# Depthwise convolution stage: shifted copies by way of HBM and 32-column matmuls for taps on VectorE and diagonal matmuls

## The chip, the cores and the metric

The kernel runs on one core of a Trainium2 chip. The metric is the device time of one execution, in microseconds (us), median of several runs. All data are float32.

## The reference, cut to what matters

The program is a chain of three small networks of 1024 features (D) over 256 tokens (T): SwiGLU blocks, several attention mixers, two mixtures of experts and one convolution block. Only the convolution block is changed. It stands between two SwiGLU blocks and adds its result to x:

```python
def rms_norm(x, g):
    y = xf * lax.rsqrt(jnp.mean(xf * xf, axis=-1, keepdims=True) + RMS_EPS)
    return y * g

def conformer_conv(h, w_pw1, b_pw1, w_dw, b_dw, ln_g, ln_b, w_pw2, b_pw2):
    val, gate = jnp.split(h @ w_pw1 + b_pw1, 2, axis=-1)
    u = val * jax.nn.sigmoid(gate)
    u = conv(u, w_dw, 31 taps, causal, one filter for each channel) + b_dw
    u = jax.nn.silu(layer_norm(u, ln_g, ln_b))
    return u @ w_pw2 + b_pw2

x = x + conformer_conv(rms_norm(x, g), ...)
```

## The kernel before, in words

x stays in SBUF with features on the partitions: 8 chunks (c) of 128 channels, 256 tokens along the free axis. The engines (TensorE `pe`, ScalarE `act`, VectorE `dve`, GpSimd `pool`, SyncE `sp`) each run their own hand-written order of work, stage by stage, and wait for each other by counting semaphores (class `Signal`).

Weights arrive in slabs of 128x2048 floats (1 MB). SyncE loads them all in one order into a ring of four (L2554); ScalarE rounds each into a high part (`round_slab`, L1352), VectorE subtracts to get the low part (`rest_slab`, L1771), and TensorE multiplies in three passes, high by high, high by low, low by high (`product`, L616 to L618), or in the SwiGLU blocks in two passes, the first with both parts of the input side by side (`product_wide`, L687 and L688). A slab can be rounded when TensorE has done with the slab three before it; both engines work two slabs ahead of TensorE. Where a slab is rounded in the order of ScalarE's and VectorE's other work is written out in each stage.

The convolution stage (`conv` of each engine) goes like this. VectorE first adds the last result of the block before to x (`finish`, L1893, once for each pair of chunks). ScalarE squares x, TensorE sums the squares over the partitions with a matrix of ones (L638), the root and its reciprocal follow (L1792, L1376, L1794), VectorE scales x (L1808), and the scaled input is split into a high part by ScalarE (L1383) and a low part by VectorE (`h_rest`, L1816). Eight slabs of w_pw1 follow (`project_slab`), each giving value and gate of one chunk in a PSUM bank; ScalarE takes the sigmoid (L1491) and VectorE makes the gated chunk u (L1997).

The 31 taps are shared out: chunks 0 to 4 go to VectorE, one 128x256 multiply-and-add for each tap (L2005 the first, L2008 the rest, 155 in all, up to 14 behind each projected slab and what is left after the last one). Chunks 5 to 7 go to TensorE as 93 matmuls of a diagonal 128x128 matrix with the shifted chunk (L866); ScalarE (L1497) and GpSimd (L2508) make the diagonals, two of three and one of three. When all is done TensorE sums the chunks for the mean (L871), VectorE subtracts it (L2019), ScalarE squares (L1504), TensorE sums again (L876), and the reciprocal root follows (L2021, L1506, L2023).

Each chunk is then scaled (L2026), put through SiLU (L1509), rounded (L1511) and its low part taken (L1816 again), one chunk after the other:

```python
for c in range(DC):
    nc.vector.tensor_tensor(v.v[:, c, :], v.v[:, c, :], v.stat[:, 1, :], ALU.mult).then_inc(k.scaled.up())
    self.h_rest(c, v.v[:, c, :], DC)
self.out_project(v, DC, "b_pw2")
```

`out_project` multiplies by w_pw2 in slabs of 256 output columns, so that each slab needs all eight chunks and finishes two chunks of x, to which VectorE adds them at once with the bias (L1831).

Three other stages already do what this change brings to the convolution. `early_input` (mixer and SwiGLU) splits the unnormed x times the gain, chunk by chunk behind `finish`, and leaves the scale by the root to the output; `add_squares` adds the squares on GpSimd so that TensorE sums only two tiles; and `mixed_half` with `add_down` multiplies by slabs of 256 input rows, so that TensorE starts with the first chunk, all eight PSUM banks are filled together and x is added by the next stage's `finish` (L1847).

## Time and profile before

| | us |
|---|---|
| runs | 4509.42, 4504.01, 4496.34 |
| median | 4504.01 |
| the profiled execution | 4514.16 |
| its span in the profile | 4512.8 |
| TensorE busy | 4261.0 (94%) |
| VectorE busy | 3007.9 (67%) |
| ScalarE busy | 1941.7 (43%) |
| GpSimd busy | 205.4 (5%) |

The mean granted clock of TensorE was 0.969 of full speed. "PE" is a matmul, "PEld" the load of its weights, "ACTq" and "SPq" are the sequencers of ScalarE and SyncE when they issue a DMA. A float32 matmul whose operands are not rounded beforehand shows as two records.

### The profile page before, as it was taken

The page shows a single profiled execution, that of the slowest core. Times are in us where ns is not written, and L with a number is a line of the kernel's source. Part 1 is how long each engine was busy: PE and PEld are TensorE (multiplying, and loading weights), DVE is VectorE, ACT ScalarE, POOL GpSimd, SP SyncE. Part 2 cuts the span into 40 slices and gives each one's busy share as a digit, 9 for nine tenths or more (in the row PEclk, how much of TensorE's full clock was granted, in tenths as well). Part 3 has the DMA queues.
Part 4 walks back from the last instruction along what each step waited for, and adds up shares of the span by engine and source line. Part 5 has one row for each costly group of instructions (what it writes and reads, how often), then busy time and mean ns, then how long its engine had stood idle before and what let it go on. Part 6 is the DMA issues. An engine that isn't in the chain of part 4 may idle for free.

```text
span 4512.8 us, 71781 instructions
## 1 busy us (share of the span) xinstructions
PE 4261.0 (94%) x30660; PEld 3934.3 (87%) x30660; DVE 3007.9 (67%) x4268; ACT 1941.7 (43%) x2485; POOL 205.4 (5%) x246
## 2 busy tenths in 40 slices
PE   7989999899998999979989999999999899999998
PEld 6878888888887888868877899999998899999998
DVE  6566675566758757557545799747755588954964
ACT  4445454454544545345435443343244444234233
POOL 0011000100002000010013000000000000000000
PEclk9989999899999999979988999999999999999999
DMA  5523545245441455414541353354353345245243
GB/s 200 183 102 141 187 168 192 85 159 187 159 159 66 174 179 185 163 65 169 181 159 38 142 186 131 132 186 141 128 186 124 125 169 186 94 170 185 103 169 140
DMA packets 94413, 677.06 MB, mean 150 GB/s; under 512 B 11264, under 2 KB 11920, under 8 KB 12816
## 3 DMA queue, kind: packets, MB, share of 16 engines
q1 hardware_dynamic: 90864, 660.64, 41.1%
q0 software_dynamic: 1024, 7.62, 0.4%
q8 instruction: 243, 3.98, 0.4%
q10 hardware_dynamic: 2208, 4.21, 0.2%
q14 instruction: 74, 0.61, 0.0%
HBM read 669.26 MB, written 3.17 MB: 149 GB/s over the span
## 4 chain that ended last, share of the span: by engine, by line
PE 80%; DVE 13%; ACT 3%; issue 1%; POOL 1%; DMA 1%; ACTq 0%; POOLq 0%; DVEq 0%; SPq 0%
PE psum L687 20%; PE psum L616 14%; PE psum L617 13%; PE psum L618 13%; PE psum L688 10%; PE psum L1331 3%; DVE slab_low L1771 3%; DVE room L2412 1%; DVE room L2008 1%; ACT slab_high L1352 1%; PE psum L1025 1%; DVE x L1893 1%; DVE room L2428 1%; DVE room L2410 1%; DVE room L2414 1%
## 5 line engine op out<-in xcount | busy, mean ns | idle before, releaser
L1771 DVE TENSOR_TENSOR slab_low<-slab,slab_high 128x2048 fp32r<-128x2048 f32 x622 | 1427.6, 2296 | 794.6 <-ACT slab_high L1352 791.8
L1352 ACT ACTIVATE slab_high<-slab 128x2048 fp32r<-128x2048 f32 x630 | 1186.3, 1883 | 511.3 <-PE psum L688 263.5
L687 PE MATMUL psum<-h_parts,slab_high 128*128 128x512 f32 x2816 | 1001.9, 401 | 42.4 <-DVE h_parts L2072 38.5
L616 PE MATMUL psum<-h_parts,slab_high 128*128 128x256 f32 x3200 | 941.0, 294 | 63.8 <-DVE h_parts L1816 38.7
L617 PE MATMUL psum<-h_parts,slab_high 128*128 128x256 f32 x3200 | 921.6, 288 | 0.0
L618 PE MATMUL psum<-h_parts,slab_low 128*128 128x256 f32 x3200 | 920.9, 288 | 0.0
L688 PE MATMUL psum<-h_parts,slab_low 128*128 128x256 f32 x2816 | 791.5, 281 | 0.0
L616 PEld LDWEIGHTS psum<-h_parts,slab_high 128*128 128x128 f32 x3200 | 630.3, 197 | 83.7 <-issue 60.3
L687 PEld LDWEIGHTS psum<-h_parts,slab_high 128*128 128x128 f32 x2816 | 532.8, 189 | 179.6 <-issue 31.5
L616 PE MATMUL psum<-hidden_parts,slab_high 128*128 128x256 f32 x2304 | 656.7, 285 | 11.5 <-DVE hidden_parts L2436 4.0
L617 PE MATMUL psum<-hidden_parts,slab_high 128*128 128x256 f32 x2304 | 647.9, 281 | 0.0
L618 PE MATMUL psum<-hidden_parts,slab_low 128*128 128x256 f32 x2304 | 646.6, 281 | 0.0
L617 PEld LDWEIGHTS psum<-h_parts,slab_high 128*128 128x128 f32 x3200 | 631.2, 197 | 2.4 <-issue 2.4
L618 PEld LDWEIGHTS psum<-h_parts,slab_low 128*128 128x128 f32 x3200 | 630.3, 197 | 0.0
L688 PEld LDWEIGHTS psum<-h_parts,slab_low 128*128 128x128 f32 x2816 | 535.0, 190 | 0.2
L687 PE MATMUL psum<-hidden_parts,slab_high 128*128 128x512 f32 x1408 | 496.2, 395 | 0.0
L616 PEld LDWEIGHTS psum<-hidden_parts,slab_high 128*128 128x128 f32 x2304 | 437.5, 190 | 20.8 <-issue 16.1
L617 PEld LDWEIGHTS psum<-hidden_parts,slab_high 128*128 128x128 f32 x2304 | 436.6, 190 | 0.0
L618 PEld LDWEIGHTS psum<-hidden_parts,slab_low 128*128 128x128 f32 x2304 | 435.9, 189 | 0.0
L688 PE MATMUL psum<-hidden_parts,slab_low 128*128 128x256 f32 x1408 | 396.4, 282 | 0.0
L687 PEld LDWEIGHTS psum<-hidden_parts,slab_high 128*128 128x128 f32 x1408 | 264.6, 188 | 63.4
L1732 ACT ACTIVATE room<-psum 128x512 f32<-128x512 f32 x128 | 76.5, 597 | 555.0 <-PE psum L618 555.0
(317 smaller groups left out, 4566.2 us busy)
## 6 DMA issues: line engine op xcount, KB each, us to landing
slab<-in_up SPq DMA_DIRECT2D x176, 1024.0 KB, 4.8
slab<-in_keys_up SPq DMA_DIRECT2D x128, 1024.0 KB, 4.8
slab<-in_keys_down SPq DMA_DIRECT2D x128, 1024.0 KB, 4.8
slab<-in_down SPq DMA_DIRECT2D x88, 1024.0 KB, 4.8
slab<-in_w_in SPq DMA_DIRECT2D x16, 1024.0 KB, 4.8
slab<-in_wq SPq DMA_DIRECT2D x16, 1024.0 KB, 4.9
slab<-in_w_pw SPq DMA_DIRECT2D x12, 1024.0 KB, 4.8
slab<-in_w_qkv SPq DMA_DIRECT2D x12, 1024.0 KB, 4.8
```

What stands on the lines that cost most here:

```text
L616: nc.tensor.matmul(out, lhs[0], rhs[0], start=first, stop=False, **options)
L617: nc.tensor.matmul(out, lhs[0], rhs[1], start=False, stop=False, **options)
L618: return nc.tensor.matmul(out, lhs[1], rhs[0], start=False, stop=last, **options)
L687: nc.tensor.matmul(out, lhs[0], rhs, start=first, stop=False, **options)
L688: return nc.tensor.matmul(out[:, 0, :], lhs[1], rhs[:, 0, :], start=False, stop=last, **options)
L1025: mm = nc.tensor.matmul(k.banks[6][:, at:at + P], v.probs[:, n % 5, e, kt * P:(kt + 1) * P], v.diagonals[:, n % 3, e, :], start=True, stop ...
L1331: mm = nc.tensor.matmul(bank[:, 2 * HALF * t:2 * HALF * (t + 1)], v.firsts[:, b % 2, t, :], v.seconds[:, b % 2, t, :], start=True, stop=True)
L1352: nc.scalar.activation(k.high[m % PARTS][:, 0:width], k.slabs[m % RING][:, 0:width], ACT.Copy).then_inc(k.rounded.up())
L1732: nc.scalar.activation(v.hidden[:, at:at + 2, :], k.banks[4 + r % 2].rearrange("p (e t) -> p e t", e=2), ACT.Gelu_apprx_tanh).then_inc(k.a ...
L1771: nc.vector.tensor_tensor(k.low[m % RING][:, 0:width], k.slabs[m % RING][:, 0:width], k.high[m % PARTS][:, 0:width], ALU.subtract).then_in ...
L1893: add = nc.vector.scalar_tensor_tensor(out=both, in0=k.bank_pairs[j][:, :, a * T:(a + 1) * T], scalar=0.5, in1=both, op0=ALU.mult, op1=ALU ...
L2008: add = nc.vector.scalar_tensor_tensor(out=dst, in0=src, scalar=w, in1=dst, op0=ALU.mult, op1=ALU.add)
```

## The change

The input is split unnormed by `early_input`; the squares are added on GpSimd; TensorE sums them after the first projected slab (bank 7). VectorE multiplies each projected bank by the reciprocal root into `raws`, makes the tap weights of one chunk in one instruction (128x1024, `weights`), and gates in place. ScalarE now waits for `raws`, takes the sigmoid, and then issues DMAs: one store of the gated chunk before to HBM (`store_lines`), and four copies back of the chunk two before (`spread_lines`). A copy puts 32 channels, shifted by 0, 8, 16 or 24 tokens, on a quarter of the partitions; the four channel groups of a chunk lie side by side on the free axis. The taps of all eight chunks are then done by TensorE: for each of 8 steps and each of 4 channel groups one matmul of 128 rows (four shifts of 32 channels) by 32 columns by 256 tokens, with the output in the group's quarter of one bank: 32 matmuls for a chunk, 256 in all. VectorE's 155 tap instructions, the 93 diagonal matmuls and the 93 diagonals are gone. The sums for the mean are spread between the chunks (`conv_sum`, two chunks behind). The output side goes by chunks (`mixed_half`), the bias is added to x beforehand, and the next SwiGLU block starts with `finish` of its four pairs.

```diff
+    c["stack"] = np.tile(np.eye(32), (4, 1))
...
-        self.first_pair = {"ffn": 0, None: 0, "mixer_one": 2}.get(before, 1)
+        self.first_pair = {"ffn": 0, None: 0, "mixer_one": 2, "conv": 2}.get(before, 1)
...
+LINE = T + 32
+STEPS = 8
...
+    v.u, v.v = k.carve(DC, LINE), k.carve(DC, T)
+    v.raws, v.stat = k.carve(2, 2, T), k.carve(2, T)
...
+    v.squares, v.rstd = k.carve(2, T), k.carve(T)
+    v.spread = k.carve(DC, 4, T + STEPS)
+    v.weights = k.carve(DC, 4 * STEPS, 32)
+    assert k.taken <= k.room_words - DC * 2 * T
+    v.mixed = k.hidden[:, FC - DC:FC]
...
     def conv(self, v):
         k, nc = self.k, self.k.nc
-        self.stage_enters(True)
-        self.norm(v)
+        self.stage_enters(False)
+        for n in range(DC):
+            if n >= 3:
+                nc.tensor.wait_ge(k.columns_scaled.sem, k.columns_scaled.at(n - 2))
+            for half in range(2):
+                self.project_half(n, half, k.banks[n % 3])
+            if n == 0:
+                nc.tensor.wait_ge(k.squares_added.sem, k.squares_added.at(3))
+                nc.tensor.wait_ge(k.move.sem, 16)
+                for a in range(2):
+                    mm = nc.tensor.matmul(k.banks[7][:, 0:T], k.const("ones"), v.squares[:, a, :], start=(a == 0), stop=(a == 1))
+                mm.then_inc(k.summed.up())
         for c in range(DC):
-            if c >= 3:
-                nc.tensor.wait_ge(k.conv_gated.sem, k.conv_gated.at(c - 2))
-            self.project_slab(c, k.banks[c % 3])
-        nc.tensor.wait_ge(k.padded.sem, k.padded.at(1))
-        n_act = n_pool = 0
-        for m in range(CONV_ON_PE * TAPS):
-            c, tap = DC - CONV_ON_PE + m // TAPS, m % TAPS
-            bank = k.banks[4 + c % 2]
-            if tap == 0:
-                nc.tensor.wait_ge(k.conv_gated.sem, k.conv_gated.at(c + 1))
...
-            if m % 3 < 2:
...
-            nc.tensor.matmul(bank[:, 0:T], v.diagonals[:, m % 4], v.u[:, c, tap:tap + T],
-                             start=(tap == 0), stop=(tap == TAPS - 1)).then_inc(k.tapped.up())
-        nc.tensor.wait_ge(k.filtered.sem, k.filtered.at((DC - CONV_ON_PE) * TAPS))
-        nc.tensor.wait_ge(k.conv_biased.sem, k.conv_biased.at(CONV_ON_PE))
-        for c in range(DC):
-            mm = nc.tensor.matmul(k.banks[4][:, 0:T], k.const("ones"), v.v[:, c, :], start=(c == 0), stop=(c == DC - 1))
-        mm.then_inc(k.conv_summed.up())
+            bank = k.banks[3 + c % 4]
+            nc.tensor.wait_ge(k.taps_made.sem, k.taps_made.at(c + 1))
+            nc.tensor.wait_ge(k.lines_spread[c].sem, k.lines_spread[c].at(4))
+            if c >= 4:
+                nc.tensor.wait_ge(k.conv_biased.sem, k.conv_biased.at(c - 3))
+            for step in range(STEPS):
+                for g in range(4):
+                    mm = nc.tensor.matmul(bank[32 * g:32 * g + 32, 0:T], v.weights[:, c, STEPS * g + step, :], v.spread[:, c, g, step:step + T],
+                                          start=(step == 0), stop=(step == STEPS - 1), tile_position=(0, 32 * g), skip_group_check=True)
+            mm.then_inc(k.tapped.up())
+            if c >= 2:
+                self.conv_sum(v, c - 2)
+        self.conv_sum(v, DC - 2)
+        self.conv_sum(v, DC - 1)
         for c in range(DC):
             if c % 2 == 0:
                 nc.tensor.wait_ge(k.squared.sem, k.squared.at(DC // 2 + c // 2 + 1))
-            mm = nc.tensor.matmul(k.banks[5][:, 0:T], k.const("ones"), v.centred_square[:, c, :], start=(c == 0), stop=(c == DC - 1))
+            mm = nc.tensor.matmul(k.banks[4][:, 0:T], k.const("ones"), v.centred_square[:, c, :], start=(c == 0), stop=(c == DC - 1))
         mm.then_inc(k.conv_summed.up())
-        self.out_project(DC)
+        for c in range(DC):
+            self.mixed_half(v, c // 2, c % 2)
+    def conv_sum(self, v, c):
+        k, nc = self.k, self.k.nc
+        nc.tensor.wait_ge(k.conv_biased.sem, k.conv_biased.at(c + 1))
+        mm = nc.tensor.matmul(k.banks[7][:, 0:T], k.const("ones"), v.v[:, c, :], start=(c == 0), stop=(c == DC - 1), skip_group_check=True)
+        if c == DC - 1:
+            mm.then_inc(k.conv_summed.up())
...
     def conv(self, v):
         k, nc = self.k, self.k.nc
-        self.stage_enters(True)
-        self.normed_input(v)
+        self.stage_enters(False)
+        self.early_input(v, k.vec("g2_0_1", 0, DC))
         for c in range(DC):
+            if c == 0:
+                self.root(v.rstd)
+            gate = v.raws[:, c % 2, 1, :]
+            nc.scalar.wait_ge(k.columns_scaled.sem, k.columns_scaled.at(c + 1))
+            nc.scalar.activation(gate, gate, ACT.Sigmoid, bias=k.vec("b_pw1", DC + c)).then_inc(k.conv_sigmoid.up())
+            if c >= 1:
+                self.store_lines(v, c - 1)
             if c >= 2:
-                nc.scalar.wait_ge(k.conv_gated.sem, k.conv_gated.at(c - 1))
...
-        for m in range(CONV_ON_PE * TAPS):
-            c, tap = DC - CONV_ON_PE + m // TAPS, m % TAPS
-            if m % 3 < 2:
...
-                nc.scalar.activation(v.diagonals[:, m % 4], k.const("ident"), ACT.Copy, scale=k.vec("w_dw", c * TAPS + tap)).then_inc(k.diagonal_act.up())
...
+                self.spread_lines(v, c - 2)
+        self.round_slab()
+        self.store_lines(v, DC - 1)
+        self.spread_lines(v, DC - 2)
+        self.spread_lines(v, DC - 1)
+        for c in range(DC):
+            nc.scalar.wait_ge(k.tapped.sem, k.tapped.at(c + 1))
+            nc.scalar.activation(v.v[:, c, :], k.banks[3 + c % 4][:, 0:T], ACT.Identity, bias=k.vec("b_dw", c)).then_inc(k.conv_biased.up())
...
-            nc.scalar.activation(k.h[:, c, 0, :], v.v[:, c, :], ACT.Copy).then_inc(k.h_rounded.up())
-        for j in range(DC // 2):
-            self.round_slab()
+            nc.scalar.activation(v.mixed[:, c, 0, :], v.v[:, c, :], ACT.Copy).then_inc(k.mixed_rounded.up())
+            if c in (3, 5, 7):
+                self.round_slab()
+    def store_lines(self, v, c):
+        k, nc = self.k, self.k.nc
+        if c == 0:
+            nc.scalar.wait_ge(k.padded.sem, k.padded.at(2))
+        nc.scalar.wait_ge(k.conv_gated.sem, k.conv_gated.at(c + 1))
+        nc.scalar.dma_start(k.dram["conv_lines"][c * P:(c + 1) * P, :], v.u[:, c, :]).then_inc(k.lines_stored[c % 2].up(), 16)
+    def spread_lines(self, v, c):
+        k, nc = self.k, self.k.nc
+        nc.scalar.wait_ge(k.lines_stored[c % 2].sem, k.lines_stored[c % 2].at(c // 2 + 1))
+        for a in range(4):
+            nc.scalar.dma_start(v.spread[32 * a:32 * a + 32, c], k.dram["conv_spread"][c][a]).then_inc(k.lines_spread[c].up(), 16)
...
-        self.stage_enters(True)
-        self.normed_input(v, "g2_0_1")
+        self.early_input(k.vec("g2_0_1", 0, DC))
-        filtered_at, n_filtered = {}, 0
         for c in range(DC):
             self.rest_slab()
+            if c == 0:
+                self.inverse_root(v.rstd, k.banks[7][:, 0:T], 1, D)
             bank = k.banks[c % 3].rearrange("p (a t) -> p a t", a=2)
+            nc.vector.wait_ge(k.slab_done.sem, k.slab_done.at(c + 1))
+            nc.vector.tensor_tensor(v.raws[:, c % 2], bank, v.rstd.unsqueeze(1).to_broadcast([P, 2, T]), ALU.mult).then_inc(k.columns_scaled.up())
+            nc.vector.tensor_tensor(v.weights[:, c], k.const("stack").unsqueeze(1).to_broadcast([P, 4 * STEPS, 32]),
+                                    k.vec("w_dw", 32 * c, 32).unsqueeze(2).to_broadcast([P, 4 * STEPS, 32]), ALU.mult).then_inc(k.taps_made.up())
+            nc.vector.scalar_tensor_tensor(out=v.u[:, c, pad:pad + T], in0=v.raws[:, c % 2, 0, :], scalar=k.vec("b_pw1", c), in1=v.raws[:, c % 2, 1, :],
...
-            for m, tap in v.taps_after.get(c, ()):
...
-                    add = nc.vector.scalar_tensor_tensor(out=dst, in0=src, scalar=w, in1=dst, op0=ALU.mult, op1=ALU.add)
-                add.then_inc(k.filtered.up())
...
+        self.rest_slab()
+        for c in range(DC):
+            x = k.x[:, c, :]
+            nc.vector.tensor_scalar(x, x, k.vec("b_pw2", c), None, ALU.add).then_inc(k.x_biased.up())
+        nc.vector.wait_ge(k.x_biased.sem, k.x_biased.at(DC))
+        nc.vector.wait_ge(k.conv_biased.sem, k.conv_biased.at(DC))
         nc.vector.wait_ge(k.conv_summed.sem, k.conv_summed.at(1))
-        self.then(nc.vector.tensor_scalar(v.stat[:, 0, :], k.banks[4][:, 0:T], 1.0 / D, None, ALU.mult))
+        self.then(nc.vector.tensor_scalar(v.stat[:, 0, :], k.banks[7][:, 0:T], 1.0 / D, None, ALU.mult))
...
         for c in range(DC):
             nc.vector.tensor_tensor(v.v[:, c, :], v.v[:, c, :], v.stat[:, 1, :], ALU.mult).then_inc(k.scaled.up())
-            self.h_rest(c, v.v[:, c, :], DC)
-        self.out_project(v, DC, "b_pw2")
+            if c >= 1:
+                self.activated_rest(v, c - 1)
+            if c in (4, 6):
+                self.rest_slab()
+        self.activated_rest(v, DC - 1)
+        self.rest_slab()
+        self.add_down(DC + DC // 2)
+    def activated_rest(self, v, c):
+        k, nc = self.k, self.k.nc
+        nc.vector.wait_ge(k.mixed_rounded.sem, k.mixed_rounded.at(c + 1))
+        nc.vector.tensor_tensor(v.mixed[:, c, 1, :], v.v[:, c, :], v.mixed[:, c, 0, :], ALU.subtract).then_inc(k.mixed_ready.up())
...
-        self.stage_enters(True)
+        self.stage_enters(False)
         nc.gpsimd.memset(v.u[:, :, 0:TAPS - 1], 0.0).then_inc(k.padded.up())
...
-                nc.gpsimd.tensor_scalar(v.diagonals[:, m % 4], k.const("ident"), k.vec("w_dw", c * TAPS + tap), None, ALU.mult).then_inc(k.diagonal_pool.up())
+        nc.gpsimd.memset(v.u[:, :, TAPS - 1 + T:LINE], 0.0).then_inc(k.padded.up())
+        self.add_squares(v)
...
+    taps = np.zeros((4 * STEPS, D), np.float32)
+    taps[0:TAPS] = i["conv_w_dw_2"][0]
+    vec["w_dw"] = taps.reshape(4, STEPS, D // 32, 32).transpose(0, 3, 2, 1).reshape(P, D // 32 * STEPS)
...
-    a["w_pw2"] = tiles(i["conv_w_pw2_2"][0])
+    a["w_pw2"] = down_slabs(i["conv_w_pw2_2"][0])
...
+    lines = nc.dram_tensor("conv_lines", [DC * P, LINE], F32)
+    dram["conv_lines"] = lines.ap()
+    dram["conv_spread"] = [[bass.AP(lines, c * P * LINE + STEPS * a, [[LINE, 32], [32 * LINE, 4], [1, T + STEPS]]) for a in range(4)] for c in range(DC)]```

ScalarE's order in the first part of the stage. `slab_high_..<-slab_..` is the rounding of a slab (L1352 before, L1358 now). Before, around the fourth to sixth projected slab:

```order
L1352 ACTIVATE slab_high_57<-slab_51 128x2048
L1491 ACTIVATE room<-psum,vectors 128x256
L1352 ACTIVATE slab_high_58<-slab_52 128x2048
L1491 ACTIVATE room<-psum,vectors 128x256
L1352 ACTIVATE slab_high_59<-slab_49 128x2048
```

Now, the last of them and what follows (L1497 is the sigmoid, L1528 the store, L1535 the copies back, L1508 the bias of the filtered chunks):

```order
L1358 ACTIVATE slab_high_57<-slab_50 128x2048
L1497 ACTIVATE room<-room,vectors 128x256
L1528 DMA conv_lines<-room 128x288
L1535 DMA room<-conv_lines 32x4x264 x4
L1358 ACTIVATE slab_high_58<-slab_51 128x2048
L1497 ACTIVATE room<-room,vectors 128x256
L1528 DMA conv_lines<-room 128x288
L1535 DMA room<-conv_lines 32x4x264 x4
L1358 ACTIVATE slab_high_59<-slab_52 128x2048
L1528 DMA conv_lines<-room 128x288
L1535 DMA room<-conv_lines 32x4x264 x8
L1508 ACTIVATE room<-psum,vectors 128x256 x8
```

Five DMA issues now stand between a sigmoid and the next rounding, and the eight bias instructions stand behind the last of the copies back.

TensorE's order after the last projected slab (L863 are the taps, L882 the sums for the mean):

```order
L863 MATMUL psum<-room 32x256 [waits lines_spread1,taps_made]
L863 MATMUL psum<-room 32x256 x31
L863 MATMUL psum<-room 32x256 [waits lines_spread2,taps_made]
L863 MATMUL psum<-room 32x256 x31
L882 MATMUL psum<-room,consts 128x256 [waits conv_biased]
L863 MATMUL psum<-room 32x256 [waits lines_spread3,taps_made]
```

The first sum stands behind the taps of the third chunk (2) and waits for the bias of the first.

## Rows read from the trace of the kernel before

**Rows 1.** Windows: stretch, busy us of PE, PEld, DVE, ACT, POOL, PEclk, DMA, GB/s.
```profile
1400.00:1440.00 40.00, 35.18 (x153) 27.64 (x153) 37.65 (x86) 19.43 (x50) 22.50 (x25) 1.00 0.00 1
1450.00:1470.00 20.00, 10.85 (x39) 8.82 (x40) 9.46 (x18) 10.43 (x18) 0.00 (x0) 0.52 0.00 1
```
**Rows 2.** The chain that ended last, 1400 to 1450 us: start, us, what.
```profile
1400.80 21.92 DVE room L2008 x53
...
1438.78 3.73 PE psum L871 x16
...
1449.23 1.76 DVE room L2023
```
**Rows 3.** Timeline, stage start and projection: start, us, engine, line.
```profile
1325.08 5.38 DVE L1893 SCALAR_TENSOR_TENSOR x<-psum,x 128x512 f32<-128x512 f32 x8
...
1364.89 0.48 ACT L1491 ACTIVATE room<-psum,vectors 128x256 f32<-128x256 f32 x1 [3.49 <-PE psum L618]
...
1370.65 0.47 ACT L1491 ACTIVATE room<-psum,vectors 128x256 f32<-128x256 f32 x1 [3.48 <-PE psum L618]
```
**Rows 4.** Timeline of the output side and the next block's start.
```profile
1453.13 0.55 PE L616 MATMUL psum<-h_parts,slab_high 128*128 128x256 f32 x1 [4.84 <-DVE h_parts L1816]
...
1466.99 0.41 PE L616 MATMUL psum<-h_parts,slab_high 128*128 128x256 f32 x1
1467.21 0.41 PE L617 MATMUL psum<-h_parts,slab_high 128*128 128x256 f32 x1
...
1488.93 0.28 PE L618 MATMUL psum<-h_parts,slab_low 128*128 128x256 f32 x1
...
1503.09 0.42 DVE L1792 TENSOR_SCALAR room<-psum 128x256 f32<-128x256 f32 x1 [4.27 <-PE psum L730]
```
**Rows 5.** Timeline of the first mixer's start: finish, DMA issues, rounding, squares on GpSimd.
```profile
219.34 1.41 DVE L1893 SCALAR_TENSOR_TENSOR x<-psum,x 128x512 f32<-128x512 f32 x2
...
221.17 0.45 ACTq L1442 DMA_DIRECT2D room<-in_w_kv_up  x1
221.65 0.45 ACTq L1443 DMA_DIRECT2D room<-in_sinks  x1
...
225.00 0.91 ACT L1553 ACTIVATE h_parts<-x,vectors 128x256 fp32r<-128x256 f32 x2 [1.88 <-DVE x L1893]
...
230.57 0.91 ACT L1553 ACTIVATE h_parts<-x,vectors 128x256 fp32r<-128x256 f32 x2 [1.88 <-DVE x L1893]
...
234.13 4.74 POOL L2460 TENSOR_TENSOR room<-room 128x512 f32<-128x512 f32 x2
```
**Rows 6.** Windows: the first mixer once TensorE has waited for those squares.
```profile
240.00:246.00 6.00, 6.00 (x28) 5.81 (x28) 2.37 (x3) 0.42 (x1) 0.00 (x0) 0.50 0.00 0
```
**Rows 7.** Groups by line: engine, shapes, count, busy us, mean ns, idle before.
```profile
L1771 DVE TENSOR_TENSOR slab_low<-slab,slab_high 128x2048 fp32r<-128x2048 f32 x622 | 1427.6, 2296 | 794.6 <-ACT slab_high L1352 791.8
L1352 ACT ACTIVATE slab_high<-slab 128x2048 fp32r<-128x2048 f32 x630 | 1186.3, 1883 | 511.3 <-PE psum L688 263.5
...
L2412 DVE TENSOR_TENSOR room<-room,consts 128x1024 f32<-128x1024 f32 x128 | 155.9, 1218 | 0.0
```
**Rows 8.** DMA issues: count, KB each, us from issue to landing.
```profile
slab<-in_up SPq DMA_DIRECT2D x176, 1024.0 KB, 4.8
...
bias_lines<-room POOLq DMA_DIRECT2D x2, 12.0 KB, 1.7
```
**Rows 9.** TensorE tiles: 64 rows by 32 columns (group); 128 by 64 (timeline, half clock).
```profile
L1150 PE MATMUL psum<-slab,room 64*32 64x128 f32 x512 | 9.8, 291 | 4.6 <-issue 4.6
...
1988.61 1.12 PE L922 MATMUL psum<-room 128*64 128x256 f32 x4
...
1989.89 0.76 PE L922 MATMUL psum<-room 128*64 128x256 f32 x4
```
**Rows 10.** Timeline where the mixer's output by chunks ends and a SwiGLU block starts.
```profile
383.99 0.28 PE L618 MATMUL psum<-hidden_parts,slab_low 128*128 128x256 f32 x1
...
400.77 0.43 DVE L1792 TENSOR_SCALAR room<-psum 128x256 f32<-128x256 f32 x1 [2.34 <-PE psum L730]
```

69 lines of the change are left out of this document (10 added, 59 removed).

## The prediction

> **What bounds the kernel now.** I read the windows over the convolution stage first, for each engine's load and TensorE's clock, then the chain of waits, then the timelines of its start and end. The stage begins when VectorE starts its last additions to x at 1325.1 us [rows 3]; I count from there. The rest of the program stays as it is, so the sum is over this stage and the first slabs of the next block.
>
> Three things set its length. First the taps: between 1400 and 1440 us VectorE is busy for 37.65 us of 40 while no slab moves (1 GB/s) [rows 1], and the chain runs through its taps, 53 of them in one piece of 21.92 us [rows 2]; TensorE, at full clock, waits for them before the first sum of 3.73 us, which ends at 1442.5 [rows 2]. So start to first sum is 117.4 us. Second the way into the output product: from its first matmul at 1453.13 to its last at 1488.93 plus one spacing, 36.0 us [rows 4]; TensorE gets a chunk only every 1.9 us at first, is busy for 10.85 of 20 us and its clock stands at 0.52, so at 1.2 GHz nearly throughout [rows 1]. Third the start, where TensorE does nothing until x is normed. In the projection itself a sigmoid follows every 5.76 us (1364.89 and 1370.65) [rows 3]: 48 matmuls at 0.12 us each, TensorE's own pace at full clock.
>
> **The start, now.** The mixer's start shows the same `early_input`. There the additions begin at 219.34; the roundings of two pairs of chunks that are two pairs apart stand at 225.00 and 230.57, so a pair takes 2.79 us; the last rounding ends at 231.48 [rows 5], 12.1 us in. 1.4 us of it are three DMA issues, two of them shown, 0.48 us apart, which the convolution doesn't have here: 10.8 us. The first slab is multiplied chunk by chunk behind that. But TensorE then waits for GpSimd's sum of squares, whose last two additions end at 238.87, 7.4 us behind the last rounding [rows 5]: 18.1 us. Two full-width matmuls (0.9 us), scale, root and reciprocal (0.43, 0.42, 1.76 [rows 2]) and VectorE's first scaled bank (0.69; eight such PSUM reads take 5.38 [rows 3]) come to 22.6 us with the gaps.
>
> The wait costs clock too. In the mixer TensorE ran at 0.50 for all of 240 to 246 us behind the same wait, though never idle in them [rows 6]. A matmul of 256 columns takes 0.21 us then (1466.99 and 1467.21 [rows 4]) instead of 0.12. For the second slab I add 3.2 us: its scaled bank is out at 28.9 us, the third's at 34.6.
>
> **The rounds, now.** From there TensorE is no longer the pace. ScalarE's order is round, sigmoid, five DMA issues, round. VectorE can't scale a bank before it has made the low part of the slab just rounded, and the sigmoid waits for that bank. So the round is a ring: rounding 1.93, low part 2.25 net of overlap [rows 7], scaled bank 0.69, five issues at 0.47 (the spacing in [rows 5]) 2.35, handovers 0.2; together 7.4 us against TensorE's 5.76. The sigmoid runs beside the first issue. The tap weights (128x1024, 1.22 us by the nearest shape [rows 7]) and the gate (0.48) lie beside the issues, so I cost them at nothing; if issues were free, VectorE's 2.25 + 0.69 + 1.22 + 0.48 = 4.6 would still fit in 5.76. The first two slabs' lead absorbs part, and five rounds at 7.4 bring the eighth scaled bank from 34.6 to 71.6 us. TensorE has projected it at 62.7 and begins the taps.
>
> Then ScalarE still has five issues (74.0), a rounding (76.0), the last store (76.4), four copies, the wait for that store to land, and four more copies: 80.5 us. For the store of 144 KB I take 2.2 us, between 1.7 for 12 KB and 4.8 for 1 MB [rows 8]. The last copies land about 3 us later, before TensorE asks for them.
>
> **The taps, now.** The bias of chunk 0 stands behind the last copy on ScalarE, and TensorE, done with three chunks, waits for it until 80.9 us. One full-width float32 matmul of 256 tokens takes 3.73 / 8 = 0.466 us [rows 2]. A chunk has 32 with 32 columns each. If the four column quarters run side by side this is 8 x 0.466 = 3.7 us a chunk, if one after the other 14.9. The trace has no float32 matmul of 128 rows by 32 columns. Nearest are: 512 records of 64 rows by 32 columns in 9.8 us busy, 19 ns each, where 128 tokens alone take 107 ns at 2.4 GHz, so more than five of eight tiles at once; and pairs of 64-column tiles at half clock, where two heads (4 records of 256 and 4 of 128 tokens) go from 1988.61 to 1989.89, 1.28 us, against 2.56 us one by one: two at once, entirely [rows 9]. I take side by side, 3.7. From 80.9: a sum 0.47, half clock after the idle stretch 2.0, five chunks with a sum each 5 x 4.16 = 20.8, two sums 0.92. The first sum ends at 105.1 us instead of 117.4: **-12.3 us.**
>
> **The end, now.** From the first sum to the first output matmul nothing changes (10.6 us); the bias is added to x while VectorE waits. The output product has 192 matmuls as before, but 24 are ready with the first chunk, and ScalarE and VectorE deliver a chunk every 1.1 us. So TensorE never starves: the first chunk at half clock 24 x 0.213 = 5.1, the other 168 at 0.12 us make 20.1, together 25.2 instead of 36.0: **-10.8 us.** The roundings that now stand between the chunks are covered by 2.9 us of matmuls a chunk. In return x is finished only behind the last matmul. From the last matmul's start to the next block's root the mixer shows 383.99 to 400.77, 16.8 us [rows 10], the convolution now 1488.93 to 1503.09, 14.2 [rows 4]: **+2.6 us.** In all -20.5 us.
>
> **Unknown costs, bounded.** A DMA issue with rows in three dimensions may cost from nothing beside other work to about 0.8 us: rounds at TensorE's pace give 9 us more, 0.8 gives 12.6 us less. A chunk's taps lie between 3.4 (+1.5 us) and 14.9. Stores of 4.8 and copies of 8 us cost 2 more. The half clock ranges over 2 us either way.
>
> **The rivals.**
> *Issues dear:* each of the 39 issues takes 0.8 us. The ring is then 9 us. For it: a copy has 128 runs of 1 KB. Against: issues of very different sizes all take 0.36 to 0.45. Gain 7.9, 4496 us.
> *Issues hidden:* ScalarE works on beside them. For it: an issue can run beside an instruction already sent. Against: the next rounding stands behind all five. Gain 29.7, 4474.
> *Tiles side by side with a toll:* the 19 ns a record are 1.4 times what eight tiles at once would give (107 / 8 = 13.4 ns) [rows 9]; if that ratio is a toll of the tiles and not of the short 128 tokens, a chunk takes 5.3 us, and five of them 8 us more. Gain 12.5, 4491. The Trainium skill ("TensorE: Matmul & The Clock Gate", Part 3: Packing small matmuls) has such a toll: three column tiles gave 2.38 times the speed of one after the other, so three lasted 1.26 times as long as one. By that ratio a chunk would be 4.7 us, as an estimate, and the sum 5 us worse; the trace bears it out for 64x32 tiles and not for the 64-column pairs.
> *Tiles half side by side:* 7.4 us a chunk, say since four moving streams compete. Gain 0, 4504. This is also the point from which the change loses.
> *Tiles one after the other:* 14.9 us a chunk; TensorE never waits for the bias. The first sum then ends at 62.7 + 8 x 14.9 + 8 x 0.47 = 185.5 us, 68 later than before: a loss of 60 us, 4564. Against it stands everything in [rows 9]; for it, that no row has all 128 rows with four quarters.
>
> **How the numbers follow.** The profiled execution took 4514.16 us, its span 4512.8; with the sum it would take 4493.7. It lies 10.2 above the median of 4504.01, within the runs' spread of 13 us; so I take the change off the median: 4483.5 us. Chances: forecast, with its bounds, 0.57 (own range 4475 to 4494); issues dear or copies late 0.12; issues hidden 0.07; tiles with a toll 0.11; half side by side 0.07; one by one 0.06. A measurement of this kernel can tell about 0.3%, 13.5 us. Faster by more: 0.52 of the forecast's 0.57, the hidden issues, and 0.06 of dear issues and toll, 0.65. Within: 0.25. Slower: 0.10, the serial tiles and what of the half-packed ones passes the bound. 4470 to 4503 leaves out two in ten.
>
> **What would show it.** In the new profile: VectorE's scaled banks 7.4 us apart in the later rounds, with ScalarE's idle time before a rounding filled by issues of 0.45; TensorE idle for some 7 us behind the third chunk's taps, until the last copy is issued; a chunk of taps in 3.7 us at full clock; first sum 105 us after the additions; output product in about 25 us. It is wrong if scaled banks stay 5.8 us apart, if a chunk's taps take over 5 us, or if the idle stretch ends with a DMA landing instead of the bias.

## The result, and the profile after

The changed kernel took 4483.15 us (median of 14 runs, 4468.47 to 4497.72); beside it the kernel before took 4504.99 (14 runs, 4490.38 to 4538.35). The ratio is 0.9942, 95% interval 0.9922 to 0.9961: 18 to 35 us faster, outside the 13.5 us that a measurement can't tell. The forecast was 4483.5. The profiled execution took 4468.47 us with a span of 4467.2. One execution of e6 below took 4805.67 us at a granted clock of 0.814; it is left out of e6's median.

That hit is better than its working. The stage, from VectorE's first addition to x to the next block's root, took 178.0 us before [rows 3, 4]; now it takes 160.8, so 17.2 us less where 20.5 were forecast. The 45.6 us between the two profiled spans are mostly not the stage's: it started 9.3 us earlier already, and executions of one kernel differ by 29 us and more. So below I compare stages, each counted from its own start, here 1315.80 us; with the median a stage is compared only where the kernels share a chip.

VectorE's line of the changed kernel at the stage's start and end, in its timeline (start, us, engine, line; in brackets the idle time before and what ended it):

```profile
1338.78 0.69 DVE L2019 TENSOR_TENSOR room<-psum,room 128x512 f32<-128x512 f32 x1
...
1344.06 0.69 DVE L2019 TENSOR_TENSOR room<-psum,room 128x512 f32<-128x512 f32 x1
...
1460.11 0.69 DVE L1869 TENSOR_TENSOR x<-psum,x 128x512 f32<-128x512 f32 x1 [1.35 <-PE psum L615]
...
1476.60 0.42 DVE L1814 TENSOR_SCALAR room<-psum 128x256 f32<-128x256 f32 x1 [2.37 <-PE psum L727]
```

L2019 is the scaled bank, L1869 the addition of the output to x, L1814 the start of the next block's root. The first bank ends 23.7 us in (forecast 22.6), the second 28.9 (28.9). Then ScalarE's timeline, parts of four of the eight rounds and the end. L1497 is the sigmoid, L1358 the rounding of a slab, L1528 the store, L1535 the copies:

```profile
1358.10 0.34 ACTq L1528 DMA_DIRECT2D conv_lines<-room  x1
1358.48 2.43 ACTq L1535 DMA_DIRECT2D room<-conv_lines  x4
1361.02 1.92 ACT L1358 ACTIVATE slab_high<-slab 128x2048 fp32r<-128x2048 f32 x1 [2.42 <-issue]
1365.89 0.51 ACT L1497 ACTIVATE room<-room,vectors 128x256 f32<-128x256 f32 x1 [2.96 <-DVE room L2019]
1365.90 0.34 ACTq L1528 DMA_DIRECT2D conv_lines<-room  x1
1366.29 4.17 ACTq L1535 DMA_DIRECT2D room<-conv_lines  x4
1370.55 1.91 ACT L1358 ACTIVATE slab_high<-slab 128x2048 fp32r<-128x2048 f32 x1 [4.15 <-issue]
1375.43 0.51 ACT L1497 ACTIVATE room<-room,vectors 128x256 f32<-128x256 f32 x1 [2.96 <-DVE room L2019]
...
1392.18 0.51 ACT L1497 ACTIVATE room<-room,vectors 128x256 f32<-128x256 f32 x1 [2.96 <-DVE room L2019]
1392.19 0.34 ACTq L1528 DMA_DIRECT2D conv_lines<-room  x1
1392.58 1.92 ACTq L1535 DMA_DIRECT2D room<-conv_lines  x4
...
1395.02 3.94 ACTq L1535 DMA_DIRECT2D room<-conv_lines  x8
1399.01 1.20 ACT L1508 ACTIVATE room<-psum,vectors 128x256 f32<-128x256 f32 x3 [2.50 <-issue]
```

The ring of waits that the prediction describes is there: sigmoid, issues, and the rounding behind the issues ("<-issue"). But four copies that should have cost 1.9 us cost 2.4, 4.2 and then 1.9 again. The last five rounds took 7.94, 7.80, 9.54, 7.60 and 9.15 us, 8.4 on average instead of 7.4.

TensorE's timeline from the third chunk's taps (L863) on; L882 is the sum that runs two chunks behind:

```profile
1399.53 1.22 PE L882 MATMUL psum<-room,consts 128*128 128x256 f32 x2 [6.64 <-ACT room L1508]
1400.68 6.01 PE L863 MATMUL psum<-room 128*32 128x256 f32 x64
1406.63 0.70 PE L882 MATMUL psum<-room,consts 128*128 128x256 f32 x2
1407.26 3.68 PE L863 MATMUL psum<-room 128*32 128x256 f32 x64
...
1419.95 3.68 PE L863 MATMUL psum<-room 128*32 128x256 f32 x64
1423.57 1.56 PE L882 MATMUL psum<-room,consts 128*128 128x256 f32 x6
```

It idles 6.64 us until ScalarE reaches the bias of chunk 0, runs one chunk at half clock (6.01 instead of 3.68), and ends the first sum at 1425.13, 109.3 us in. It had also waited once in the projection, 3.56 us for a slab's low part (until 1374.94), and its clock stood at 0.83 in 1370 to 1380. The windows over the output side answer to the second one of [rows 1] (columns as there):

```profile
1435.00:1440.00 5.00, 4.30 (x23) 4.33 (x24) 2.71 (x7) 2.82 (x7) 0.00 (x0) 0.66 0.00 0
1440.00:1445.00 5.00, 5.00 (x45) 5.00 (x44) 0.00 (x0) 1.79 (x1) 0.00 (x0) 1.00 0.14 31
1445.00:1450.00 5.00, 5.00 (x44) 5.00 (x44) 3.73 (x5) 3.18 (x6) 0.00 (x0) 1.00 0.57 198
```

TensorE is never starved, and its clock is full again (1.00) before the first chunk's 24 matmuls are done; the product, with its first matmul at 1435.70, takes 24.2 us instead of 36.0 [rows 4].

### The profile page after: what moved, and what is told of

It is laid out like the page before. It is cut to its first block, busy times and chain, and to the rows that moved or that the text cites. A ratio compares the mean times of both kernels' runs of the same rounds, so it can differ in the third digit from the quotient of the medians.

```text
span 4467.2 us, 72221 instructions
## 1 busy us (share of the span) xinstructions
PE 4217.0 (94%) x30974; PEld 3891.5 (87%) x30974; DVE 2955.3 (66%) x4125; ACT 1921.3 (43%) x2428; POOL 184.1 (4%) x219
## 4 chain that ended last, share of the span: by engine, by line
PE 80%; DVE 13%; ACT 4%; issue 1%; POOL 1%; DMA 1%; ACTq 1%; POOLq 0%; DVEq 0%; SPq 0%
PE psum L684 20%; PE psum L613 14%; PE psum L615 13%; PE psum L614 13%; PE psum L685 10%; PE psum L1337 3%; DVE slab_low L1793 3%; ACT slab_high L1358 1%; DVE room L2441 1%; PE psum L1031 1%; DVE x L1915 1%; POOL room L2489 1%; DVE room L2457 1%; DVE room L2439 1%; DVE room L2443 1%
## 5 line engine op out<-in xcount | busy, mean ns | idle before, releaser
L1358 ACT ACTIVATE slab_high<-slab 128x2048 fp32r<-128x2048 f32 x630 | 1186.5, 1883 | 515.4 <-PE psum L685 259.4
L613 PE MATMUL psum<-h_parts,slab_high 128*128 128x256 f32 x3136 | 918.4, 293 | 50.8 <-DVE h_parts L2101 22.2
L614 PE MATMUL psum<-h_parts,slab_high 128*128 128x256 f32 x3136 | 899.9, 287 | 0.0
L615 PE MATMUL psum<-h_parts,slab_low 128*128 128x256 f32 x3136 | 899.1, 287 | 0.0
L685 PE MATMUL psum<-h_parts,slab_low 128*128 128x256 f32 x2816 | 790.6, 281 | 0.0
L613 PE MATMUL psum<-hidden_parts,slab_high 128*128 128x256 f32 x2368 | 671.9, 284 | 16.4 <-DVE hidden_parts L2057 4.8
L684 PEld LDWEIGHTS psum<-h_parts,slab_high 128*128 128x128 f32 x2816 | 531.7, 189 | 177.4 <-issue 32.8
L613 PEld LDWEIGHTS psum<-h_parts,slab_high 128*128 128x128 f32 x3136 | 614.9, 196 | 68.3 <-issue 53.1
L614 PE MATMUL psum<-hidden_parts,slab_high 128*128 128x256 f32 x2368 | 661.8, 279 | 0.0
L615 PE MATMUL psum<-hidden_parts,slab_low 128*128 128x256 f32 x2368 | 661.6, 279 | 0.0
L614 PEld LDWEIGHTS psum<-h_parts,slab_high 128*128 128x128 f32 x3136 | 614.8, 196 | 2.5 <-issue 2.4
L615 PEld LDWEIGHTS psum<-h_parts,slab_low 128*128 128x128 f32 x3136 | 613.9, 196 | 0.0
L685 PEld LDWEIGHTS psum<-h_parts,slab_low 128*128 128x128 f32 x2816 | 534.8, 190 | 0.2
L613 PEld LDWEIGHTS psum<-hidden_parts,slab_high 128*128 128x128 f32 x2368 | 449.4, 190 | 26.0 <-issue 21.3
L615 PEld LDWEIGHTS psum<-hidden_parts,slab_low 128*128 128x128 f32 x2368 | 449.2, 190 | 0.0
L614 PEld LDWEIGHTS psum<-hidden_parts,slab_high 128*128 128x128 f32 x2368 | 449.0, 190 | 0.0
L685 PE MATMUL psum<-hidden_parts,slab_low 128*128 128x256 f32 x1408 | 396.4, 282 | 0.0
L684 PEld LDWEIGHTS psum<-hidden_parts,slab_high 128*128 128x128 f32 x1408 | 264.6, 188 | 63.3
## 6 DMA issues: line engine op xcount, KB each, us to landing
slab<-in_up SPq DMA_DIRECT2D x176, 1024.0 KB, 4.8
slab<-in_keys_up SPq DMA_DIRECT2D x128, 1024.0 KB, 4.8
slab<-in_keys_down SPq DMA_DIRECT2D x128, 1024.0 KB, 4.8
slab<-in_down SPq DMA_DIRECT2D x88, 1024.0 KB, 4.8
slab<-in_w_in SPq DMA_DIRECT2D x16, 1024.0 KB, 4.8
slab<-in_wq SPq DMA_DIRECT2D x16, 1024.0 KB, 4.8
slab<-in_w_pw SPq DMA_DIRECT2D x12, 1024.0 KB, 5.2
slab<-in_w_qkv SPq DMA_DIRECT2D x12, 1024.0 KB, 4.8
```

Of the source, the lines that this page charges most:

```text
L613: nc.tensor.matmul(out, lhs[0], rhs[0], start=first, stop=False, **options)
L614: nc.tensor.matmul(out, lhs[0], rhs[1], start=False, stop=False, **options)
L615: return nc.tensor.matmul(out, lhs[1], rhs[0], start=False, stop=last, **options)
L684: nc.tensor.matmul(out, lhs[0], rhs, start=first, stop=False, **options)
L685: return nc.tensor.matmul(out[:, 0, :], lhs[1], rhs[:, 0, :], start=False, stop=last, **options)
L1358: nc.scalar.activation(k.high[m % PARTS][:, 0:width], k.slabs[m % RING][:, 0:width], ACT.Copy).then_inc(k.rounded.up())
```

## The experiments

My theory: the gain is that of the output by chunks and of taps off VectorE; what is missing to the forecast lies in ScalarE's queue, where the copies' issues slow the loop and the biases stand behind the last of them. The rival: the DMA engines or TensorE set this pace, and ScalarE's issues only fill time. The runs' medians and ratios to the kernel before (of their own batch), and, read from each profile and counted in us from the stage's start, the end of the first sum and the stage's length:

| run | median us | ratio (95%) | first sum ends | stage |
|---|---|---|---|---|
| kernel before | 4504.99 | 1 | 117.4 | 178.0 |
| changed | 4483.15 | 0.9942 (0.9922 to 0.9961) | 109.3 | 160.8 |
| e1 copies by GpSimd | 4478.23 | 0.9908 (0.9873 to 0.9942) | 95.1 | 148.7 |
| e2 bias by VectorE | 4487.31 | 0.9928 (0.9903 to 0.9952) | 107.8 | 159.3 |
| e3 roundings last | 4487.41 | 0.9918 (0.9892 to 0.9945) | 108.0 | 159.4 |
| e4 one quarter | 4565.31 | 1.0092 (1.0063 to 1.0120) | 183.6 | 237.3 |
| e5 output side back | 4497.88 | 0.9956 (0.9936 to 0.9977) | 108.2 | 168.0 |
| e6 normed input back | 4491.72 | 0.9942 (0.9921 to 0.9962) | 105.2 | 158.7 |
| e7 copies in pairs | 4484.61 | 0.9919 (0.9891 to 0.9948) | 101.7 | 155.2 |
| e8 biases ahead of copies | 4488.91 | 0.9918 (0.9888 to 0.9947) | 104.6 | 156.0 |
| e9 changed, again | 4486.98 | 0.9947 (0.9928 to 0.9967) | 107.7 | 159.2 |
| e10 e1, sum by VectorE | 4471.51 | 0.9912 (0.9893 to 0.9930) | 91.1 | 144.6 |
| e11 e10, normed input | 4476.66 | 0.9927 (0.9908 to 0.9945) | 92.0 | 145.1 |
| e12 biases ahead of rounding | 4485.62 | 0.9942 (0.9922 to 0.9962) | 104.2 | 155.7 |

The stage of the unaltered kernel came out at 160.8 and 159.2, and in the eight profiles with its start and loop (those two, e2 to e5, e8 and e12) the eighth scaled bank ended between 73.0 and 76.3 us. So a difference under some 3 us in the stage says nothing by itself. The intervals of the ratios overlap, and alone would not order e1 to e3. e1 to e4 shared a chip, e5 to e8 and e9 to e12 likewise; the kernel before took 4523.06, 4513.48 and 4508.11 us in these batches.

**e1, who issues the copies.**

```diff
-            if c >= 2:
-                self.spread_lines(v, c - 2)
...
+        for c in range(DC):
+            nc.gpsimd.wait_ge(k.lines_stored[c].sem, k.lines_stored[c].at(1))
+            for a in range(4):
+                nc.gpsimd.dma_start(v.spread[32 * a:32 * a + 32, c], k.dram["conv_spread"][c][a]).then_inc(k.lines_spread[c].up(), 16)
```

The signals for a stored line, two that are used in turn in the changed kernel, become eight.

> The changed kernel with the 32 spreading copies issued by GpSimd instead of ScalarE; the eight stores stay on ScalarE. In the changed kernel a round of the projection loop took 8.4 us (five issues by ScalarE in it 2.3 to 4.5 us) and the stage 160.8 us. Theory A, the time in which ScalarE issues paces the rounds: they fall to 5.5 to 6.2 us, the eighth scaled bank comes 60 to 64 us after the stage's start instead of 76, and the stage takes 145 to 152 us. Theory B, the DMA engines are the pace (busy 0.84 to 0.90 in these windows) and an issue is long only because the queue behind it is full: the wait moves to the arrival of the weight slab, rounds stay at 8.0 us or more, and the stage stays within 3 us of 160.8. A third way: GpSimd's own issues are slow (over 1.2 us each, four a chunk), the taps then wait for the last copies, and the gain is under half of A's.

GpSimd's and TensorE's timelines:

```profile
1372.91 2.18 POOL L2526 DMA_DIRECT2D room<-conv_lines  x4 [3.17 <-DMA conv_lines<-room]
...
1376.79 10.62 PE L863 MATMUL psum<-room 128*32 128x256 f32 x192
1387.35 0.70 PE L882 MATMUL psum<-room,consts 128*128 128x256 f32 x2
1387.97 3.69 PE L863 MATMUL psum<-room 128*32 128x256 f32 x64
```

The windows from the first bank to the first sum, columns as in [rows 1]:

```profile
1338.00:1377.00 39.00, 39.00 (x328) 38.82 (x331) 31.45 (x30) 16.49 (x14) 10.99 (x20) 1.00 0.78 248
1377.00:1388.00 11.00, 11.00 (x198) 7.14 (x190) 6.52 (x12) 3.77 (x5) 3.09 (x6) 1.00 0.66 195
1388.00:1410.00 22.00, 22.00 (x335) 12.23 (x334) 0.00 (x0) 2.37 (x5) 3.43 (x7) 1.00 0.21 51
```

The later rounds alone, first in the changed kernel, then in e1:

```profile
1350.00:1392.00 42.00, 38.44 (x405) 34.89 (x407) 22.07 (x21) 12.12 (x10) 0.00 (x0) 0.96 0.74 230
1350.00:1377.00 27.00, 27.00 (x228) 26.82 (x231) 21.29 (x20) 11.19 (x9) 9.09 (x17) 1.00 0.97 309
```

All that theory A forecast came. The last rounds fall to 5.76 us, which is TensorE's own pace, the eighth scaled bank ends at 62.5 us instead of 76.3, the idle stretch and the half clock ahead of the first sum are gone, and TensorE is busy all the time from the first bank to the first sum. So the DMA engines were not the pace of the changed kernel: there they were busy for 0.74 of the later rounds at 230 GB/s, and in e1 they moved 309. But they are busy for 0.97 in e1, which leaves them little room for shorter rounds. GpSimd pays 0.54 us an issue (2.18 for four), steadily. The Trainium skill ("DMA: Bandwidth & Descriptors", Issuing engines are not separate DMA queues) says that issuing from several engines only saves the sequencer's issue time, usually small beside the transfer. The saving here is of that kind, since the bytes are the same and moved faster only as the rounds became shorter. Yet it was 12.1 us of the stage (10.5 against e9's), since the sequencer belonged to the engine on the critical ring.

**e2, biases on VectorE.**

```diff
-            nc.scalar.activation(v.v[:, c, :], k.banks[3 + c % 4][:, 0:T], ACT.Identity, bias=k.vec("b_dw", c)).then_inc(k.conv_biased.up())
+            nc.vector.tensor_scalar(v.v[:, c, :], k.banks[3 + c % 4][:, 0:T], k.vec("b_dw", c), None, ALU.add).then_inc(k.conv_biased.up())
```

> The changed kernel with the eight convolution biases computed by VectorE, which is idle there, instead of by ScalarE behind its last copies. Theory A, TensorE's 6.6 us of idle time and the half-clock taps after it come from the order of ScalarE's queue: the idle time goes, the first sum ends 6 to 9 us earlier than 109.4 us after the stage's start, and the stage takes 152 to 155 us instead of 160.8. Theory B, the taps would wait for their copies anyway: TensorE idles at the copies of chunk 3 to 5, the first sum ends within 2 us of 109.4.

A miss. TensorE's and VectorE's timelines there:

```profile
1396.19 2.29 DVE L1790 TENSOR_TENSOR slab_low<-slab,slab_high 128x2048 fp32r<-128x2048 f32 x1 [2.86 <-ACT slab_high L1358]
1398.40 2.19 DVE L2027 TENSOR_SCALAR x<-x,vectors 128x256 f32<-128x256 f32 x8
1400.50 1.26 DVE L2030 TENSOR_SCALAR room<-psum,vectors 128x256 f32<-128x256 f32 x3
...
1401.04 1.22 PE L882 MATMUL psum<-room,consts 128*128 128x256 f32 x2 [8.75 <-DVE room L2030]
```

VectorE was idle, but its queue was not free: the biases stood behind a low part that waits for ScalarE's last rounding and behind eight additions to x. One wait took the other's place, 8.75 us for 6.64. The first sum, at 107.8, came within theory B's 2 us, but not by B's reason: no copy's landing ends a wait of TensorE. Neither theory had what happened.

**e8 and e12, the same wait by order alone.** e8 moves ScalarE's biases 0 to 2 ahead of the last eight copies, e12 ahead of the last rounding and store too. This is e12's edit; in e8 the rounding and the store stay where they were:

```diff
-        self.round_slab()
-        self.store_lines(v, DC - 1)
-        self.spread_lines(v, DC - 2)
-        self.spread_lines(v, DC - 1)
         for c in range(DC):
+            if c == 3:
+                self.round_slab()
+                self.store_lines(v, DC - 1)
+                self.spread_lines(v, DC - 2)
+                self.spread_lines(v, DC - 1)
```

> The changed kernel with ScalarE's biases of chunks 0 to 2 put ahead of its last eight copies. The run with the biases on VectorE kept TensorE's idle time, 8.8 us, since VectorE came to them only behind its last slab rounding and the eight additions to x. Theory A, the idle time is ScalarE's or VectorE's order and nothing else: here chunk 3's taps start about 1 us after chunk 2's, the clock stays full, the first sum ends 7 to 9 us earlier than in the changed kernel (about 101 us) and the stage takes 151.5 to 154 us. Theory B, the taps of chunks 3 to 7 wait for their copies, which this edit delays by 1.4 us: first sum after 106 us, stage over 157 us.

> The changed kernel with ScalarE's biases of chunks 0 to 2 ahead of its last slab rounding, store and copies. With the biases between that rounding and the copies TensorE still idled 5.5 us, of which the rounding was the last 1.9 us. Theory A, the order of ScalarE's queue is all of the idle time: TensorE idles 2.5 us or less between chunk 2's and chunk 3's taps, keeps its full clock, the first sum ends 101 to 103 us after the stage's start, and the stage takes 151 to 154 us. Theory B, the last chunks' copies, now 3 us later, hold the taps up: stage over 156 us.

TensorE's longest wait fell from 6.64 us (7.8 in e9) to 5.5 and 3.35. In e12:

```profile
1399.89 1.22 PE L882 MATMUL psum<-room,consts 128*128 128x256 f32 x2 [3.35 <-ACT room L1509]
1401.04 5.85 PE L863 MATMUL psum<-room 128*32 128x256 f32 x64
```

The stage came to 156.0 and 155.7, in each case between my two theories. Since the loop ahead of it varies, what the order is worth is better counted from the eighth scaled bank to the end of the first sum: 33.0 and 33.1 us in the changed kernel (e9 is the second), 34.9 in e2, 30.0 in e8, 28.4 in e12. The copies don't hold the taps up (no wait for a landing in either), so the order of work on the engine that does the biases is the cause. But 3.35 us are left in e12. Of them 0.43 pass until the eighth bank is scaled, which the sigmoid ahead of the first bias needs, 0.43 in the sigmoid's start and the store's issue, 1.91 in the issues of chunk 5's copies, which still stand ahead of that bias, and 0.58 in the bias itself and the handovers. The clock fell all the same. Only e1, e4, e10 and e11, without such an idle stretch, kept it over the taps.

**e7, price by the issue or by the byte.** One copy for two chunks:

```diff
-            if c >= 2:
-                self.spread_lines(v, c - 2)
+            if c in (3, 5, 7):
+                self.spread_lines(v, c // 2 - 1)
...
-    dram["conv_spread"] = [[bass.AP(lines, c * P * LINE + STEPS * a, [[LINE, 32], [32 * LINE, 4], [1, T + STEPS]]) for a in range(4)] for c in range(DC)]
+    dram["conv_spread"] = [[bass.AP(lines, 2 * j * P * LINE + STEPS * a, [[LINE, 32], [32 * LINE, 8], [1, T + STEPS]]) for a in range(4)] for j in range(DC // 2)]
```

> The changed kernel with one copy for two chunks of lines: 16 copies of twice the size instead of 32, the same bytes, all by ScalarE. Theory A, ScalarE pays by the issue (0.48 us, and more where it meets a slab's issue): two rounds together lose four issues, the eighth scaled bank comes at 66 to 70 us instead of 72 to 76, and the stage takes 151 to 156 us. Theory B, it pays by the byte or for full queues: each of the 16 copies takes twice as long, 1.0 us and more, and the stage is within 2 us of 160.8.

Theory A. The first and the last four issues in ScalarE's timeline:

```profile
1362.67 2.06 ACTq L1535 DMA_DIRECT2D room<-conv_lines  x4
...
1397.54 1.82 ACTq L1535 DMA_DIRECT2D room<-conv_lines  x4
```

The four groups of issues took 2.06, 3.20, 2.17 and 1.82 us, where eight groups of the changed kernel took 1.76 to 4.17: a copy of 264 KB is issued in about the time of one of 132. Rounds without copies took 5.3 us, rounds with them 7.4 and 8.6, and the eighth bank ended at 66.4.

**e4, side by side.** All four groups on TensorE's first quarter of columns:

```diff
-                    mm = nc.tensor.matmul(bank[32 * g:32 * g + 32, 0:T], v.weights[:, c, STEPS * g + step, :], v.spread[:, c, g, step:step + T],
-                                          start=(step == 0), stop=(step == STEPS - 1), tile_position=(0, 32 * g), skip_group_check=True)
+                    mm = nc.tensor.matmul(bank[0:32, 0:T], v.weights[:, c, STEPS * g + step, :], v.spread[:, c, g, step:step + T],
+                                          start=(step == 0 and g == 0), stop=(step == STEPS - 1 and g == 3), tile_position=(0, 0), skip_group_check=True)
```

> The changed kernel with all four groups of channels put on the first quarter of TensorE's columns (output rows 32 to 127 of every chunk are not computed). Theory A, tiles in different column quarters run side by side: here a chunk's 32 matmuls take about four times 3.61 us, 14 to 15 us at full clock, eight of them push the first sum back by 60 to 90 us, and the kernel is 1.3 to 2 per cent slower than the changed kernel. Theory B, 3.61 us is what 32 small matmuls cost in any place: nothing changes, within 2 us in the stage.

```profile
1387.18 41.64 PE L863 MATMUL psum<-room 128*32 128x256 f32 x192
...
1429.39 14.00 PE L863 MATMUL psum<-room 128*32 128x256 f32 x64
```

14.00 us a chunk against 3.68: four quarters side by side are 3.8 times as fast as one after the other. The stage is 76.5 us longer. The toll that I had weighed is not there: the Trainium skill ("TensorE: Matmul & The Clock Gate", Part 3: Packing small matmuls) has 2.38 times for three column tiles, and by that ratio a chunk would take 4.7 us, as an estimate; the measured 3.68 decides.

**e5, the output side.**

```diff
-        for c in range(DC):
-            self.mixed_half(v, c // 2, c % 2)
+        self.out_project(DC)
...
-    a["w_pw2"] = down_slabs(i["conv_w_pw2_2"][0])
+    a["w_pw2"] = tiles(i["conv_w_pw2_2"][0])
```

> The changed kernel with the output side of the kernel before (eight 256-column slabs by output pairs, x added pair by pair, next block entered as before), all else as changed. Theory A, the two halves of the change are worth what their stretches show: the output product goes from 24.2 back to 36 us and the way to the next block from 16.8 to 14.2, so the stage takes 169 to 171 us instead of 160.8, with the first sum at 105 to 110 us as now. Theory B, the output side gave less than its stretches show because the next block starts later for it: the stage takes under 165 us.

The stage took 168.0, a microsecond under A. From the first sum on it needs 59.8 us against 51.5 in the changed kernel: the chunks are worth 8.3 us, near the 9.1 that the two stretches give (11.7 less in the product, 2.6 more behind it). TensorE's half clock is back too; a window of it, beside [rows 1]:

```profile
1445.00:1455.00 10.00, 6.00 (x21) 4.82 (x22) 3.47 (x9) 4.09 (x9) 0.00 (x0) 0.50 0.00 0
```

**e6 and e11, the unnormed input.**

```diff
-        self.early_input(v, k.vec("g2_0_1", 0, DC))
+        self.normed_input(v)
```

> The changed kernel with the block's input normed before it is projected, as in the kernel before (the scaled bank becomes a plain copy). Theory A, the early start is worth the distance of the first banks (first scaled bank 23.0 us after the stage's start against the first sigmoid at 39.8 in the kernel before), the loop of eight rounds behind it runs at its own pace: the stage takes 175 to 179 us. Theory B, the loop catches up, since weight slabs are loaded meanwhile: under 170 us.

The largest miss: 158.7 us, if anything less than the changed kernel's, and the sum at 105.2. VectorE in e6 (stage start 1321.14; L2012 is the copy that stands for the scaled bank):

```profile
1321.14 5.38 DVE L1909 SCALAR_TENSOR_TENSOR x<-psum,x 128x512 f32<-128x512 f32 x8
...
1343.34 0.69 DVE L2012 COPY room<-psum 128x512 f32<-128x512 f32 x1 [4.00 <-PE psum L616]
...
1349.10 0.69 DVE L2012 COPY room<-psum 128x512 f32<-128x512 f32 x1 [0.39 <-PE psum L616]
```

The first bank is out 22.9 us in, against 23.7 with the unnormed input. I had read the sigmoid at 1364.89 of [rows 3] as the first of the kernel before; it is the fourth. The first, in ScalarE's timeline of the kernel before, starts 22.5 us in:

```profile
1347.61 0.47 ACT L1491 ACTIVATE room<-psum,vectors 128x256 f32<-128x256 f32 x1 [5.65 <-PE psum L618]
```

So there was nothing to win at this place: the additions to x take 5.4 us in one piece instead of 9.9 in turn with ScalarE, no sum of squares on GpSimd stands in the way (TensorE waits 5.5 us for it in the changed kernel), and TensorE's first product runs through. That the slow loop alone hid a gain was still possible:

> The kernel of the run before with the input normed before it is projected. With the copies on ScalarE the normed input cost nothing: its first bank was ready 22.2 us after the stage's start against 23.0, since x is finished 4.6 us sooner and TensorE's first product, though at half clock, runs without a stop. My expectation there had taken the kernel before's fourth sigmoid (39.8 us) for its first (22.5 us). Theory A, the two starts are worth the same, and TensorE sets the pace behind either: the stage within 1.5 us of the run before's. Theory B, the early input was worth its earlier second and third banks and only the slow loop hid it: 3 us or more over the run before's.

145.1 against 144.6: theory A. The unnormed input is worth nothing that the stage shows in either loop. The median of e11 is 5.2 us above that of e10; the intervals of the two ratios overlap, and no stretch that I compared accounts for it.

**e3, the roundings in the output side.**

```diff
-            if c in (3, 5, 7):
-                self.round_slab()
+        for _ in range(3):
+            self.round_slab()
```

> The changed kernel with the three roundings of weight slabs in the output side moved behind the eighth chunk, on ScalarE and VectorE. Theory A, the one stall of 3.6 to 4.8 us in the output product comes from the rounding that waits for the first output slab with four chunks' work queued behind it: the output product takes 19.5 to 21 us instead of 24.2, the rest stays, stage 156 to 157.5 us. Theory B, TensorE's half clock at that place and the order of the slabs take the gain back: the output product within 1 us of 24.2, or the next block's start is late by the same amount.

Theory B, and for a plainer reason: the stall was not there. I had placed two waits of the profile wrongly: 3.6 us are in the projection, where TensorE outruns the ring, and 4.8 stand ahead of the first output matmul. The first addition to x starts 24.4 us behind that matmul in both kernels; TensorE is the pace, as the windows above show for the changed kernel.

**e9 and e10, the measure and the best version.** e10 adds to e1:

```diff
-            if c >= 2:
-                self.conv_sum(v, c - 2)
...
+            nc.vector.tensor_tensor(v.squares[:, 0, :], v.v[:, 0, :] if c == 1 else v.squares[:, 0, :], v.v[:, c, :], ALU.add).then_inc(k.conv_added.up())
```

> The changed kernel itself, unaltered, on the same chip as the three kernels that follow, as their measure. Its stage took 160.8 us; ScalarE's issues made the eighth scaled bank come between 72 and 76 us after the stage's start in five profiles with the same loop, so the stage should take 157 to 162 us, and the median lies 15 to 35 us under that of the kernel before.

> The kernel with the copies issued by GpSimd, and with the eight filtered chunks added up by VectorE (idle there) and one matmul for their sum instead of eight. Theory A, with the copies off ScalarE, TensorE alone sets the end (it had no idle time from the first bank to the first sum): seven matmuls of 0.63 us less and one addition of 0.42 more behind the last bias, the first sum at 91 to 92 us instead of 95.2, the stage 144 to 145.5 instead of 148.7. Theory B, something else stands right behind TensorE (a copy's landing, the clock): the stage within 1 us of 148.7.

e9's stage took 159.2, within the 157 to 162 expected. In e10 TensorE does all its taps in one piece:

```profile
1375.75 26.41 PE L863 MATMUL psum<-room 128*32 128x256 f32 x484
1403.23 0.70 PE L867 MATMUL psum<-room,consts 128*128 128x256 f32 x2 [1.06 <-DVE room L2015]
```

The first sum comes some 4 us earlier than in e1 and the stage is 4.1 shorter, 144.6, as theory A had it: with the copies gone from ScalarE, TensorE alone sets this end. On the same chip e10's median is 15.5 us under e9's (4471.51 against 4486.98), where the stages differ by 14.6. It beats both kernels, the one before by 32 to 48 us.

## Why the prediction was right, and where not

*Start.* Last rounding at 10.8 us and GpSimd's squares at 18.1, both as forecast. The two matmuls of the sum took 2.07 us, at half clock, for which I had 0.9 at full clock, so the first bank came 1.1 us late; it cost nothing, the second and third came at 28.9 and 34.3 (forecast 28.9 and 34.6). The term was right in itself and no source of gain. The prediction names the start as the third thing that sets the stage's length, and that is wrong: the kernel before had its first sigmoid 22.5 us in, and e6 and e11 lose nothing without the early input.

*Rounds.* The step that failed: "five issues at 0.47 (the spacing in [rows 5]) 2.35". Rounding, low part, bank and handovers came as forecast; the 24 copies in the loop took 17.1 us together, 0.71 each, and the eighth bank came at 76.3 instead of 71.6. With the store's 0.34 that is 3.2 us a round where the ring had 2.35. The two issues of rows 5 are no fair sample: they are of 96 and 4 KB, alone but for a slab of half the size that SyncE issued 0.4 us ahead of the first (at 220.77). The rival of dear issues, at 0.8 for each, had the size of a copy nearly right and that of a store (0.34) not; its ring of 9 us lies 0.6 above the measured 8.4, the forecast's 7.4 lies 1.0 below. Its reason, the shape of the copy, does not suffice: four of the same shape took 1.92 us where SyncE had issued nothing for 8 us. What made them dear goes with the slabs beside them, as far as the last section can tell.

*Last copies.* The last copy was issued at 83.2 (forecast 80.5): 4.7 us inherited from the rounds, 2.0 given back since the last rounding ran beside the issues and not ahead of them. TensorE's 6.6 us of waiting for the bias are as foreseen, "some 7".

*Taps.* 3.68 a chunk against 3.7, and 14.00 if serial (14.9 in the rival): right. Bias to first sum took 26.1 instead of 24.2: the half clock cost 2.3 us in the chunk and 0.5 in the sum where I had 2.0, and each other sum took 0.63 for 0.47.

*First sum.* 109.3 for 105.1: -8.1 us instead of -12.3.

*Output side.* Middle 10.6 as before. Product 24.2 (forecast 25.2), from its first matmul to its last 24.1 instead of 35.8: -11.7, the clock was back before the first chunk was done. Next block +2.6, to the tenth of a us: 1459.80 to 1476.60. e5 comes within a us of this sum.

*In all* -17.2 for -20.5. That the median agrees within 0.4 us is chance on top: it fell by 21.8. e9, with a stage 18.8 us shorter than in the one profile of the kernel before, fell by 21.1 on its chip.

*The rival of hidden issues* gave 29.7 us, and e1 reaches 29.3: it was the price of the same ring without the issues. So of what the change could give, 12 us stay in ScalarE's queue: 13.8 at the eighth bank, 14.3 at the first sum, less 1.7 in the middle, where e1's clock was lower, and 0.4 behind it.

## What to carry to other kernels

Put a DMA's issue on an engine for whom nothing on the critical ring waits; on an engine of the ring each issue costs its time in full (0.71 us a copy in this loop), by the number of copies and not by their bytes (132 against 264 KB, e7). When work is moved to an idle engine, look at what stands ahead of it in that engine's order: idle time is mostly a wait, and the moved work waits with it (e2). And before giving an early start a worth, look for the first event in both kernels, not the first one in a window (e6).

## What was not expected of the hardware

ScalarE's issue of a copy has no fixed price. In the nine profiles with 32 single copies by ScalarE, the four copies of the round issued 8 us or more after SyncE's last slab issue took 1.91 or 1.92 us every time. In the rounds within 5.6 us of a slab issue they took 1.92 to 5.61; the three longest (5.61, 4.27, 4.17) had a slab issue 0.2 us into them (the first two) or 0.85 us ahead. In one, a single issue took 2.26 us. But e6 has four copies in 1.97 us with a slab issue 0.7 us into them. So slabs issued and loaded at that time go with the price and do not fix it. Whether it is the issuing itself or the full queues behind it stays open; no run separates them. GpSimd's issues stayed at 0.54, four of them 2.18 to 2.29, with slabs issued as close by.

In e1 stores landed after 6.5 us instead of 3.3 and copies after 4.6 instead of 3.8 (medians of their groups in e1 and in the changed kernel). TensorE waited for none of them. It need not be GpSimd's issuing: ScalarE still issues the stores, and the DMA engines are busy for 0.97 of the rounds. The last eight copies, behind the last slab's issue by 10 us and more, landed after 2.8 to 3.4 us in e1 and 3.2 to 3.9 in the changed kernel.

In e1 and e10 TensorE had run at full clock without a stop for some 70 us, and yet its clock fell to half about 1 us into the second sum, behind a pause of 2 us (0.81 in 1410 to 1415 in e1), where the changed kernel kept 1.00 after the same pause. The second sum took 5.41 us instead of 3.72, 1.7 more in the middle. The same happened in e4, e6, e7 and e11, and not in e2, e3, e5, e8, e9 and e12. e6 and e7 had waited 7.7 and 5.2 us for a bias before, so the long stretch without a stop is not its condition. I have no run that explains it.
